# Row statistics gathered four chunks at a time, and an earlier bf16 copy for half of the second FFN's weights, in a macaron conformer layer on eight cores

## The chip, the cores and the metric

One Trainium2 chip, all 8 cores. Each core computes one of the 8 batch rows; the cores exchange nothing. The metric is the device time of the slowest core, in microseconds (us). Engines are named as in the profile: PE (TensorE), DVE (VectorE), ACT (ScalarE), POOL (GpSimd) and SP (SyncE); the last two mostly issue transfers (DMAs).

## What is computed

x is 8 x 4096 x 1024 in float32, the layer has one level, and every product sums over the channels:

```
h = h + 0.5 * swiglu(rmsnorm(h), w_gate, w_up, w_down)        # FFN 1, width 2816
u = rmsnorm(h);  z = u @ w_in                                 # 1024 -> 7 * 1024
a = a_val * sigmoid(a_gate)
a = silu(layernorm(causal_depthwise_conv31(a) + b)) @ a_w_out
y = (b_B * causal_depthwise_conv3(b_C * b_x)) @ b_w_out
h = h + (sigmoid(g_a) * a + sigmoid(g_b) * y) @ w_o           # the mixer
h = h + 0.5 * swiglu(rmsnorm(h), ...)                         # FFN 2, width 2816
out = rmsnorm(h)
```

Both FFNs and the mixer have float32 weights of their own, which the kernel uses as bf16.

## The kernel before

**Tiles.** The 4096 positions of a core are 8 tiles of 512. A tile lives transposed: 8 chunks of 128 channels x 512 positions. For every tile there are three pieces of work: FFN 1, the mixer and FFN 2. `units` (in `_run`) lists the FFN units in the order (0,1), (1,1), (2,1), (3,1), (0,2), (4,1), (1,2), (5,1), (2,2), ... where (t,2) is FFN 2 of tile t. `gen_b` walks these units, `gen_a` the first part of the mixer (input projection, convolutions) and `gen_c` its second part. A planner in `_run` chooses at each step which of the three goes on. It carries a clock per engine in a `Tracker`: each operation is recorded with a cost (`cost=`), and a step is taken when its operands are ready by those clocks. The order of every engine's instructions is thus fixed when the program is built, and a changed cost can move the work of all three generators. All operations are issued from one helper, so the profile gives them one line (L416); they are told apart by the names of their tiles.

**Matrix products.** `group` is a chain of 128x128x512 matmuls into one of 8 PSUM banks `ps`. An FFN unit has 22 gate/up steps (16 matmuls each, moving operand `uF`) and 8 down steps (22 matmuls each, moving operand `act`). Products of the mixer read `uM`, `bact` and halves of `acc`.

**Weights.** They come in slabs of 128 x 2048 elements (128 x 1408 for the down projections, `dn1` and `dn2`, two slabs for a step; 128 x 1024 for a third of `win`) into 9 slots `wslot`. A slab is read anew for each tile. At first it is read from the float32 array `wpack` and cast on the way, by a DMA of POOL's queue. At one of its uses the slot is also written back to the array `wbf` in bf16 by a DMA of SP's queue, and from then on it is read from there, by SP's queue and with half the bytes. `write_use` says at which use that happens, counted from 0: for `gu2` and `dn2`, the slabs of FFN 2, it is 1, the second use. FFN 2 of tile 0 thus reads 38 slabs in float32, FFN 2 of tile 1 reads them in float32 again and writes all of them back, and tile 2 is the first to read them in bf16. `slab_at` issues the loads ahead, as slots come free in order, and `_writeback` the copies; a slot that is being written back can't be loaded before that copy has landed. Of the copies, four can be on their way: the fifth makes SP wait for the first.

**Row statistics.** An RMSNorm needs the sum of squares over all 8 chunks. `norm_square` has ACT square one chunk (128 x 512) into one of 7 buffers `sq`, and puts `stat` into the queue `late`. When the planner's clock says that the square is ready, `flush` calls it: `strips` issues four matmuls of PE, which sum the chunk over its channels. They have 32 columns of ones as the weight (`ones`), 128 positions each, and stand in four column groups of the array (`tile_position`), 128*32 in the profile's form. After the eighth chunk `root` makes 1/sqrt, `spread` broadcasts it with 8 matmuls on `sel`, and ACT copies it to `rstdX` or `rstdM`, which DVE multiplies into `uF` or `uM`. `ln_stat` does the same for the mixer's LayerNorm, with a square and a copy of each finished `acc`. The four strips of one chunk between two runs of full matmuls are called a visit here. `norm_square` is called for the next unit's input in `prepare` (14 units), after each down step in `gen_b` (15 units), and for the first and the last unit in other places.

Of the kernel before, what the change touches and what calls it, by code (L numbers as in the profile page):

```python
# [130 lines left out]
NCAST = 4  # L131
NSQ = 7
NACC = 12
# [196 lines left out]
class Norm:  # L330
    def __init__(self, rstd):
        self.rstd = rstd
        self.ps = None
        self.done = False

# [11 lines left out]
class Builder:  # L347
# [206 lines left out]
    def write_use(self, kk):  # L554
        if kk[0] in ("gu1", "dn1"):
            return 0 if kk[1] % 6 == 0 else 1
        if kk[0] in ("gu2", "dn2"):
            return 1
        return 2 if kk[1] % 3 == 1 else 1
# [172 lines left out]
    def new_sq(self):  # L732
        while len(self.late) >= NSQ - 1:
            self.late.popleft()[1]()
        return self.r_sq.next()

    def strips(self, ps, sq, ap, first, last):
        q = ap.shape[1] // 4
        for g in range(4):
            self.tr.op("pe", lambda E: E.matmul(  # L740
                ps.ap[32 * g:32 * g + 32, 0:q], lhsT=self.ones[:, 0:32], rhs=ap[:, g * q:(g + 1) * q],
                start=first, stop=last, tile_position=(0, 32 * g)),
                reads=[self.b_ones, sq], writes=([ps] if first and g == 0 else []), mark=(g == 3), cost=40.0)
        ps.w = ("pe", self.tr.cnt["pe"])
        ps.tw = self.tr.t["pe"] + 200.0
# [30 lines left out]

    def norm_square(self, norm, k, src, on_dve=False):
        tr = self.tr
        if k == 0:
            norm.ps = self.bank(hold=True)  # L780
        sq = self.new_sq()
# [6 lines left out]
        def total(hl):  # L788
            self.spread(norm.ps, hl, QT)
            tr.op("act", lambda E: E.activation(out=norm.rstd.ap, in_=norm.ps.ap, func=AF.Copy),  # L790
                  reads=[norm.ps], writes=[norm.rstd], cost=600)
            self.release(norm.ps)
            norm.finish()

        def stat():
            self.strips(norm.ps, sq, sq.ap, k == 0, k == KC - 1)
            if k == KC - 1:
                hl = self.root(norm.ps, QT)
                self.late.append((tr.ready([hl]), lambda: total(hl)))
        self.late.append((tr.ready([sq]), stat))  # L800

# [143 lines left out]
    def gen_b(self):  # L945
# [3 lines left out]
        for k in range(KC):  # L949
            self.norm_square(n, k, self.b_h[0][k], on_dve=(k % 2 == 1))  # L950
            self.flush()
# [52 lines left out]
    def last_down(self, q, t, h):  # L1004
# [13 lines left out]
        for es, d in steps:  # L1018
# [27 lines left out]
            self.late.append((tr.ready([sq]), stat))  # L1046
            if es == (1,):
# [67 lines left out]
    def mixer(self, t):  # L1115
# [6 lines left out]
        self.conv_left[t] = KC  # L1122
        self.ln_left[t] = 2 * KC
        for j in range(KC):
# [50 lines left out]
    def merge_out(self, t):  # L1175
# [45 lines left out]
        if t == NT - 1:  # L1221
            q = 2 * NT - 1
            h = self.b_h[q % NH]
            for i in range(KC):
# [7 lines left out]
                    reads=[ps, h[i]], writes=[h[i]], cost=690)  # L1232
                self.norm_square(self.norm_1[q], i, h[i])
            self.m_out.add(t)
# [49 lines left out]
    def ln_stat(self, t, j, acc):  # L1284
        tr = self.tr
        if j == 0:
            self.ln_ps[t] = (self.bank(hold=True), self.bank(hold=True))
        S = self.ln_ps[t]

        def stat(ps, b):  # L1290
            self.strips(ps, b, b.ap, j == 0, j == KC - 1)
            self.ln_left[t] -= 1
        sq = self.new_sq()
        tr.op("act", lambda E: E.activation(out=sq.ap, in_=acc.ap, func=AF.Square), reads=[acc], writes=[sq], cost=620)
        self.late.append((tr.ready([sq]), lambda: stat(S[1], sq)))
        cp = self.new_sq()
        tr.op("act", lambda E: E.activation(out=cp.ap, in_=acc.ap, func=AF.Copy), reads=[acc], writes=[cp], cost=620)
        self.late.append((tr.ready([cp]), lambda: stat(S[0], cp)))

    def layer_norm(self, t, acc, aact):  # L1300
# [21 lines left out]
        def second():  # L1322
# [3 lines left out]
            for ps, x in ((S1, lnr), (S0, nmr)):  # L1326
                hl = self.split(x, QT)
                self.late.append((tr.ready([hl]), lambda ps=ps, hl=hl: out(ps, hl)))

# [49 lines left out]
```

How the kernel before makes its waits and increments, by code:

```python
    def _waits(self, eng, reads, writes):  # L214
        toks = {}
        for b in reads:
            if b.w is not None:
                toks[b.w[0]] = max(toks.get(b.w[0], 0), b.w[1])
        for b in writes:
            if b.w is not None:
                toks[b.w[0]] = max(toks.get(b.w[0], 0), b.w[1])
            for t in b.r:
                toks[t[0]] = max(toks.get(t[0], 0), t[1])
        E = self.eng[eng]
        wd = self.waited[eng]
        for sk in sorted(toks):
            val = toks[sk]
            if sk == "pe" and eng == "pe":
                continue
            if wd.get(sk, 0) < val:
                E.wait_ge(self.sem[sk], val)
                wd[sk] = val
# [16 lines left out]
    def op(self, eng, fn, reads=(), writes=(), cost=700.0, mark=True, bg=False, actset=None):  # L249
        if eng == "dve" and not bg and self.fill is not None:
            self.fill(self.ready(reads, writes))
        reads, writes = _flat(reads), _flat(writes)
        self._waits(eng, reads, writes)
        ins = fn(self.eng[eng])
        if mark:
            self.cnt[eng] += 1
            ins.then_inc(self.sem[eng], 1)
            tok = (eng, self.cnt[eng])
        else:
            tok = (eng, self.cnt[eng] + 1)
# [44 lines left out]
    def wait_tok(self, eng, tok):  # L305
        if self.waited[eng].get(tok[0], 0) < tok[1]:
            self.eng[eng].wait_ge(self.sem[tok[0]], tok[1])
            self.waited[eng][tok[0]] = tok[1]
# [14 lines left out]
                def then_inc(_s, sem, val=1):  # L323
                    entry[3].append((sem, val))
```

## Time and profile before

| | us |
|---|---|
| median of 3 runs | 3174.65 (3174.19 to 3315.42) |
| the profiled execution | 3173.24 |
| its span, from the first to the last instruction, slowest core (4) | 3171.7 |
| spans of the 8 cores | 3153.5 to 3171.7 |
| PE busy, of the span | 3076.1 (97%) |
| DVE busy | 2370.8 (75%) |
| ACT busy | 891.5 (28%) |

All rows below are of core 4. A matmul is drawn from its start to a modelled end, 0.38 us for 512 columns, though the next one can start after 0.216 us; so PE can be called busy for a part of a time in which it starts nothing. "DMA" is the mean busy share of the core's 16 DMA engines, and the share of a queue is that of its packets on the same engines. Sizes of the transfers are those of the bf16 or float32 data at the destination.

### The profile page before, as it was taken

To read this page: it belongs to the slowest core of one execution; us is meant where nothing else is said; L and a number is where in the kernel's file an instruction comes from. 1 tells how busy PE (TensorE), PEld (TensorE's weight loads), DVE (VectorE), ACT (ScalarE), POOL (GpSimd) and SP (SyncE) were. 2 spreads that over 40 slices of the span, in tenths; PEclk is the share of its full clock that TensorE was granted. 3 is DMA by queue.
4 is the path that set the end of the run, shared out by engine and by line. 5 is a ranking of instruction groups with operands and counts; after the bars stand their busy time and mean duration, and the time that the engine had idled before them with its cause. 6 is when DMAs were issued, how large, how long until landed. Compare 5 with 4: busy or idle time off the path is not lost.

```text
span 3171.7 us, 48577 instructions; the slowest of 8 cores (3153.5 to 3171.7 us)
## 1 busy us (share of the span) xinstructions
PE 3076.1 (97%) x15640; PEld 1374.2 (43%) x15640; DVE 2370.8 (75%) x3511; ACT 891.5 (28%) x1648; POOL 193.2 (6%) x367
## 2 busy tenths in 40 slices
PE   8989999999989999889999999999999999999998
PEld 3434344444434444334444444444444444444444
DVE  2258898969877889668897989888988599874222
ACT  2222233224312333113323242233232422332221
POOL 1111001001110000000001000000000000000000
PEclk8999999999999999999999999999999999999999
DMA  9999959979999679997466465565574755646452
GB/s 181 186 219 206 251 141 192 216 219 208 189 209 233 209 190 251 226 234 246 148 186 227 138 220 170 169 230 156 157 232 148 228 174 162 209 147 204 126 194 92
DMA packets 182551, 612.59 MB, mean 193 GB/s; under 512 B 20768, under 2 KB 22944, under 8 KB 176544
## 3 DMA queue, kind: packets, MB, share of 16 engines
q1 hardware_dynamic: 134688, 431.58, 42.9%
q0 software_dynamic: 46640, 176.15, 28.3%
q8 instruction: 133, 2.18, 0.3%
q10 hardware_dynamic: 976, 1.74, 0.2%
q14 instruction: 114, 0.93, 0.1%
HBM read 620.89 MB, written 103.81 MB: 228 GB/s over the span
## 4 chain that ended last, share of the span: by engine, by line
PE 82%; DMA 14%; DVE 2%; issue 1%; ACT 0%; SPq 0%; DVEq 0%; POOL 0%; ACTq 0%; POOLq 0%
PE ps L416 82%; DMA wslot<-wpack 6%; DMA wbf<-wslot 3%; DMA hst<-hs 3%; DMA hs<-hst 1%; DVE acc L416 1%; DMA hT<-xT 0%; DMA wslot<-wbf 0%; SPq L416 0%; DVE hT L416 0%; ACT sq L416 0%; DVE uF L416 0%; DVE fp L416 0%; ACT L416 0%; DVE uM L416 0%
## 5 line engine op out<-in xcount | busy, mean ns | idle before, releaser
L416 DVE SCALAR_TENSOR_TENSOR acc<-abuf,vecs_sb,acc 128x512 f32<-128x512 f32 x1920 | 1435.2, 748 | 132.9 <-ACT acc L416 8.8
L416 PE MATMUL ps<-uF,wslot 128*128 128x512 bf16 x5632 | 1256.4, 381 | 22.1 <-DMA wslot<-wpack 12.9
L416 PEld LDWEIGHTS ps<-uF,wslot 128*128 128x128 bf16 x5632 | 541.8, 98 | 673.3 <-issue 42.3
L416 PE MATMUL ps<-uM,wslot 128*128 128x512 bf16 x3584 | 800.3, 380 | 8.0 <-DVE acc L416 4.6
L416 PE MATMUL ps<-act,wslot 128*128 128x512 bf16 (+1 forms) x2904 | 635.1, 376 | 15.1 <-DMA wslot<-wpack 15.1
L416 ACT ACTIVATE fp<-ps 128x512 f32<-128x512 f32 (+1 forms) x513 | 293.8, 575 | 1024.6 <-PE ps L416 997.0
L416 PEld LDWEIGHTS ps<-uM,wslot 128*128 128x128 bf16 x3584 | 346.1, 98 | 423.1 <-issue 14.7
L416 DVE TENSOR_TENSOR act<-fp,ps 128x512 bf16<-128x512 f32 x352 | 239.9, 684 | 266.1 <-PE ps L416 248.0
L416 PEld LDWEIGHTS ps<-act,wslot 128*128 128x128 bf16 x2904 | 278.2, 98 | 332.7 <-issue 25.8
L416 ACT ACTIVATE sq<-hT 128x512 bf16<-128x512 f32 (+1 forms) x256 | 157.2, 619 | 601.0 <-DVE hT L416 585.4
L416 PE MATMUL ps<-acc,wslot 128*128 128x512 bf16 x1024 | 241.2, 381 | 4.0 <-DVE acc L416 2.3
L416 POOL DMA_DIRECT2D wslot<-wpack x247 | 130.5, 530 | 1255.6 <-PE ps L416 803.6
L416 DVE SCALAR_TENSOR_TENSOR hT<-ps,hT 128x512 f32<-128x512 f32 (+1 forms) x140 | 94.2, 673 | 148.3 <-PE ps L416 148.0
L416 PEld LDWEIGHTS ps<-acc,wslot 128*128 128x128 bf16 x1024 | 97.6, 98 | 120.7 <-issue 6.7
L416 ACT ACTIVATE thg<-ps 128x512 f32<-128x512 f32 x128 | 75.1, 595 | 218.7 <-PE ps L416 191.3
L416 DVE SCALAR_TENSOR_TENSOR fp<-thg,ps 128x512 f32<-128x512 f32 x128 | 87.3, 684 | 52.3 <-PE ps L416 51.3
L416 PE MATMUL ps<-bact,wslot 128*128 128x512 bf16 x512 | 120.9, 379 | 0.0
L416 ACT ACT_TABLE_LOAD x79 | 101.4, 1283 | 65.7 <-PE ps L416 44.8
L416 PE MATMUL ps<-sq,ones 128*32 128x128 bf16 (+1 forms) x1568 | 78.0, 228 | 30.0 <-ACT sq L416 30.0
L416 ACT ACTIVATE sq<-acc 128x512 bf16<-128x512 f32 x128 | 73.5, 621 | 119.0 <-DVE acc L416 118.9
L416 PEld LDWEIGHTS ps<-sq,ones 128*32 128x32 bf16 x1568 | 34.1, 94 | 157.3 <-issue 157.1
L416 DVE SCALAR_TENSOR_TENSOR fp<-cx,vecs_sb,fp 128x512 f32<-128x512 f32 x128 | 95.3, 745 | 0.0
(57 smaller groups left out, 963.9 us busy)
## 6 DMA issues: line engine op xcount, KB each, us to landing
wslot<-wbf SPq DMA_DIRECT2D x470, 512.0 KB, 4.5
wslot<-wpack POOLq DMA_DIRECT2D x170, 512.0 KB, 15.4
wslot<-wbf SPq DMA_DIRECT2D x195, 352.0 KB, 3.3
wbf<-wslot SPq DMA_DIRECT2D x80, 512.0 KB, 11.0
wslot<-wpack POOLq DMA_DIRECT2D x61, 352.0 KB, 15.8
outT<-hT POOLq DMA_DIRECT2D x14, 1024.0 KB, 7.6
hst<-hs POOLq DMA_DIRECT2D x56, 256.0 KB, 5.4
hst<-hs SPq DMA_DIRECT2D x48, 256.0 KB, 7.6
```

What stands on the lines that cost most here:

```text
L416: ins = getattr(E, meth)(*a, **kw)
```

## The change

Four things are changed.

- **Four chunks per visit.** `norm_square` keeps the chunks and calls the new `quad` after each fourth one. `quad` takes 4 `sq` buffers, has ACT do the 4 squares one after the other, and queues one `stat` that issues 16 strips in a row. `ln_stat` does so for its copies and its squares. The ring `sq` grows from 7 to 9 buffers; `new_sqs` counts the buffers that queued visits hold. The first unit's norm, the one in the last `wo` steps (`plain=True`) and the end (`last_down`) stay as they were.
- **Costs that the planner assumes.** A strip 14 ns (40 before) and 190 ns per visit (none before), a matmul of `spread` 72 ns (90 before). They put work in another order, on all engines.
- **A `fill` call** ahead of `root`, which lets queued DVE work go first while the statistics are on their way.
- **Write-back of FFN 2.** `write_use` is `kk[1] % 2`: slabs with an even number (11 of the 22 `gu2`, 8 of the 16 `dn2`) are written back at their first use, in FFN 2 of tile 0, and read in bf16 from tile 1 on. The others stay as they were.

```diff
-NSQ = 7
+NSQ = 9
+NQ = 4
@@ write_use
         if kk[0] in ("gu2", "dn2"):
-            return 1
+            return kk[1] % 2
@@ Builder
+    def new_sqs(self, n):
+        while sum(x[2] for x in self.late) + n > NSQ:
+            self.late.popleft()[1]()
+        return [self.r_sq.next() for _ in range(n)]
+
+    def quad(self, ps, srcs, func, first, last, then):
+        tr = self.tr
+        sq = self.new_sqs(NQ)
+        for b, src in zip(sq, srcs):
+            tr.op("act", lambda E: E.activation(out=b.ap, in_=src.ap, func=func), reads=[src], writes=[b], cost=620)
+
+        def stat():
+            tr.t["pe"] += 190.0
+            for n, b in enumerate(sq):
+                self.strips(ps, b, b.ap, first and n == 0, last and n == NQ - 1)
+            then()
+        self.late.append((max(tr.ready([b]) for b in sq), stat, NQ))
@@ strips
-                reads=[self.b_ones, sq], writes=([ps] if first and g == 0 else []), mark=(g == 3), cost=40.0)
+                reads=[self.b_ones, sq], writes=([ps] if first and g == 0 else []), mark=(g == 3), cost=14.0)
@@ spread
-                    reads=[self.b_sel, hl], writes=([ps] if n == 0 else []), mark=(n == 7), cost=90.0)
+                    reads=[self.b_sel, hl], writes=([ps] if n == 0 else []), mark=(n == 7), cost=72.0)
@@ norm_square
+        def then():
+            if k == KC - 1:
+                self.fill(tr.ready([norm.ps]) + 400.0)
+                hl = self.root(norm.ps, QT)
+                self.late.append((tr.ready([hl]), lambda: total(hl), 1))
+        if not plain:
+            norm.src.append(src)
+            if k % NQ == NQ - 1:
+                self.quad(norm.ps, norm.src[-NQ:], AF.Square, k < NQ, k == KC - 1, then)
+            return
@@ ln_stat
+        if j % NQ == NQ - 1:
+            for ps, func in zip(self.ln_ps[t], (AF.Copy, AF.Square)):
+                self.quad(ps, self.ln_src[-NQ:], func, j < NQ, j == KC - 1, done)
```

Three places of the instructions' order. First PE, in the down steps of FFN 2 of tile 2 (matmuls on `act`), with the norm of the result; `sq,ones` are strips. Before:

```order
523 L416 MATMUL ps<-act,wslot 128x512 x44
524 L416 MATMUL ps<-sq,ones 32x128 x4
525 L416 MATMUL ps<-act,wslot 128x512 x22
526 L416 MATMUL ps<-sq,ones 32x128 x4
527 L416 MATMUL ps<-act,wslot 128x512 x22
528 L416 MATMUL ps<-sq,ones 32x128 x4
529 L416 MATMUL ps<-act,wslot 128x512 x22
530 L416 MATMUL ps<-sq,ones 32x128 x12
```

The same place now:

```order
331 L418 MATMUL ps<-uF,wslot 128x512 x112
332 L418 MATMUL ps<-uM,wslot 128x512 x40
333 L418 MATMUL ps<-uF,wslot 128x512 x32
334 L418 MATMUL ps<-uM,wslot 128x512 x40
335 L418 MATMUL ps<-act,wslot 128x512 x110
336 L418 MATMUL ps<-sq,ones 32x128 x16
337 L418 MATMUL ps<-act,wslot 128x512 x66
```

The strips of four chunks stand in one visit after the fifth down step, where there was a visit for almost every step. Over the whole program the runs of strips go from 300 to 108, with 1568 strips in both.

Second PE again, where the mixer of tile 2 (`uM`) hands over to FFN 2 of tile 0 (the run on `uF`); `sq,sel` is `spread`, and the one right ahead of `uF` is of a norm. Before:

```order
206 L416 MATMUL ps<-uM,wslot 128x512 x16
207 L416 MATMUL ps<-sq,sel 128x128 x8
208 L416 MATMUL ps<-uM,wslot 128x512 x24
209 L416 MATMUL ps<-sq,ones 32x128 x4
210 L416 MATMUL ps<-uM,wslot 128x512 x40
211 L416 MATMUL ps<-sq,sel 128x128 x8
212 L416 MATMUL ps<-uF,wslot 128x512 x96
```

The same place now:

```order
122 L418 MATMUL ps<-uM,wslot 128x512 x40
123 L418 MATMUL ps<-sq,sel 128x128 x8
124 L418 MATMUL ps<-uM,wslot 128x512 x24
125 L418 MATMUL ps<-sq,ones 32x128 x16
126 L418 MATMUL ps<-uM,wslot 128x512 x40
127 L418 MATMUL ps<-sq,sel 128x128 x8
128 L418 MATMUL ps<-uF,wslot 128x512 x96
```

The two norms that end here are those of FFN 1 of tile 3 (for `rstdM`) and of FFN 2's input (for `rstdX`, which `uF` needs). Before, the `spread` for `rstdX` was the first one, with 64 matmuls on `uM` between it and the run on `uF`; now it is the second one, with none between.

Third SP's queue from the load of x for the unit after next (`hT<-xT`), early in FFN 2 of tile 0, up to the loads of h's chunks (`hst<-hs`); `wbf<-wslot` is a write-back. Before:

```order
99 L416 DMA hT<-xT 128x4096
100 L416 DMA wbf<-wslot 128x2048
101 L416 DMA wslot<-wbf 128x2048
102 L416 DMA wslot<-wbf 128x1024
103 L416 DMA wbf<-wslot 128x2048 x5
104 L416 DMA wslot<-wbf 128x2048
105 L416 DMA wbf<-wslot 128x2048
106 L416 DMA wslot<-wbf 128x1024
107 L416 DMA wbf<-wslot 128x2048 x7
108 L416 DMA hst<-hs 128x512 x4
```

The same place now:

```order
107 L418 DMA hT<-xT 128x4096
108 L418 DMA wbf<-wslot 128x2048 x8
109 L418 DMA wslot<-wbf 128x2048
110 L418 DMA wbf<-wslot 128x2048
111 L418 DMA wslot<-wbf 128x1024
112 L418 DMA wbf<-wslot 128x2048 x4
113 L418 DMA wslot<-wbf 128x2048
114 L418 DMA wbf<-wslot 128x2048 x2
115 L418 DMA wslot<-wbf 128x1024
116 L418 DMA wbf<-wslot 128x2048 x8
117 L418 DMA wslot<-wbf 128x2048
118 L418 DMA wbf<-wslot 128x2048
```

Between the load of x and the first `hst` load there are 24 write-backs where there were 14. The whole program has 120 write-backs in both; loads from `wpack` go from 247 to 228 and those from `wbf` from 713 to 732.

## Rows read from the trace of the kernel before

**Rows 1.** Windows: length, busy us of PE, PEld, DVE, ACT, POOL (instructions), PE clock, DMA share, GB/s.

```profile
0.00:363.20 363.20, 322.88 (x1580) 138.15 (x1581) 192.62 (x290) 87.44 (x163) 47.83 (x94) 0.96 1.00 200
363.20:751.30 388.10, 387.73 (x1997) 173.73 (x1995) 330.26 (x485) 116.99 (x217) 27.98 (x53) 1.00 0.82 203
751.30:994.70 243.40, 225.82 (x1132) 99.91 (x1129) 198.57 (x295) 67.09 (x122) 30.08 (x57) 0.97 1.00 202
...
1163.00:1425.60 262.60, 241.87 (x1193) 105.67 (x1191) 199.53 (x297) 69.58 (x130) 19.53 (x37) 0.97 0.95 239
1425.60:3171.70 1746.10, 1731.10 (x8896) 782.45 (x8892) 1309.94 (x1944) 501.01 (x921) 61.43 (x114) 1.00 0.56 180
```

**Rows 2.** Waits of PE over the span: us in total, times, longest.

```profile
PE ps L416 <- ACT sq L416: 30.0, 10, 11.6
PE ps L416 <- DMA wslot<-wpack: 29.7, 21, 5.6
```

**Rows 3.** Timeline of PE, 1840 to 1960 us: start, length, operation.

```profile
1843.66 17.44 PE L416 MATMUL ps<-uF,wslot 128*128 128x512 bf16 x80
1860.94 1.06 PE L416 MATMUL ps<-sq,sel 128*128 128x128 bf16 x16
...
1901.76 1.89 PE L416 MATMUL ps<-bact,wslot 128*128 128x512 bf16 x8
1903.58 0.35 PE L416 MATMUL ps<-sq,ones 128*32 128x128 bf16 x12
1903.86 3.63 PE L416 MATMUL ps<-uM,wslot 128*128 128x512 bf16 x16
```

**Rows 4.** Timeline of PE, 2430 to 2470 us.

```profile
2442.86 4.92 PE L416 MATMUL ps<-act,wslot 128*128 128x512 bf16 x22
2447.71 0.29 PE L416 MATMUL ps<-sq,ones 128*32 128x128 bf16 x8
2447.94 4.92 PE L416 MATMUL ps<-act,wslot 128*128 128x512 bf16 x22
2452.79 0.24 PE L416 MATMUL ps<-sq,ones 128*32 128x128 bf16 x4
2452.96 4.92 PE L416 MATMUL ps<-act,wslot 128*128 128x512 bf16 x22
```

**Rows 5.** DMA queues and issues (last number: us to landing), 751.3 to 994.7 us.

```profile
q0 software_dynamic: 8517, 28.38, 72.7%
q1 hardware_dynamic: 6658, 20.49, 26.7%
...
wbf<-wslot SPq DMA_DIRECT2D x17, 512.0 KB, 11.1
```

**Rows 6.** DMA queues, 1163 to 1425.6 us.

```profile
q1 hardware_dynamic: 14400, 44.54, 52.3%
q0 software_dynamic: 5677, 18.01, 42.0%
```

**Rows 7.** Waits of POOL, 1163 to 1425.6 us.

```profile
POOL wslot L416 <- DMA wbf<-wslot: 142.3, 17, 22.1
```

**Rows 8.** Timeline of all engines, 915 to 945 us.

```profile
929.19 0.75 DVE L416 SCALAR_TENSOR_TENSOR uM<-hst,vecs_sb,rstdM 128x512 bf16<-128x512 f32 x1 [12.05 <-DMA hst<-hs]
...
936.27 0.30 PE L416 MATMUL ps<-sq,ones 128*32 128x128 bf16 x4 [11.58 <-ACT sq L416]
```

**Rows 9.** Timeline of all engines, 736 to 763 us.

```profile
745.44 0.61 PE L416 MATMUL ps<-sq,sel 128*128 128x128 bf16 x8
...
750.85 0.74 DVE L416 SCALAR_TENSOR_TENSOR uF<-hT,vecs_sb,rstdX 128x512 bf16<-128x512 f32 x1
...
758.41 2.07 DVE L416 SCALAR_TENSOR_TENSOR uF<-hT,vecs_sb,rstdX 128x512 bf16<-128x512 f32 x3
...
760.42 2.75 PE L416 MATMUL ps<-uF,wslot 128*128 128x512 bf16 x12
```

**Rows 10.** Groups by form: busy us, mean ns; idle before.

```profile
L416 ACT ACTIVATE sq<-hT 128x512 bf16<-128x512 f32 x248 | 153.8, 625 | 579.2 <-DVE hT L416 563.6 <-DMA hT<-xT 10.2 <-DMA hT<-hs 5.0
```

More of the change, by code:

```diff
@@ L333, in __init__ @@
         self.ps = None
+        self.src = []
         self.done = False
@@ L732, in new_sq @@
     def new_sq(self):
-        while len(self.late) >= NSQ - 1:
+        return self.new_sqs(1)[0]
+    def new_sqs(self, n):
+        while sum(x[2] for x in self.late) + n > NSQ:
             self.late.popleft()[1]()
-        return self.r_sq.next()
+        return [self.r_sq.next() for _ in range(n)]
[10 more added lines that the diff above has]
+        self.late.append((max(tr.ready([b]) for b in sq), stat, NQ))
     def strips(self, ps, sq, ap, first, last):
@@ L775, in root, with norm_square @@
         return self.split(sd, q)
-    def norm_square(self, norm, k, src, on_dve=False):
+    def norm_square(self, norm, k, src, on_dve=False, plain=False):
         tr = self.tr
@@ L780, in norm_square, with total @@
             norm.ps = self.bank(hold=True)
+        def total(hl):
+            self.spread(norm.ps, hl, QT)
+            tr.op("act", lambda E: E.activation(out=norm.rstd.ap, in_=norm.ps.ap, func=AF.Copy),
+                  reads=[norm.ps], writes=[norm.rstd], cost=600)
+            self.release(norm.ps)
+            norm.finish()
+        def then():
[8 more added lines that the diff above has]
+            return
         sq = self.new_sq()
@@ L786, in norm_square @@
             tr.op("act", lambda E: E.activation(out=sq.ap, in_=src.ap, func=AF.Square), reads=[src], writes=[sq], cost=620)
[L788 to L793, printed above, removed]
         def stat():
+            tr.t["pe"] += 190.0
             self.strips(norm.ps, sq, sq.ap, k == 0, k == KC - 1)
[L797 to L800, printed above, removed]
+            then()
+        self.late.append((tr.ready([sq]), stat, 1))
     def scale_op(self, out, src, vcol, k, norm):
@@ L949, in gen_b @@
         for k in range(KC):
-            self.norm_square(n, k, self.b_h[0][k], on_dve=(k % 2 == 1))
+            self.norm_square(n, k, self.b_h[0][k], on_dve=(k % 2 == 1), plain=True)
             self.flush()
@@ L1045, in stat @@
                     self.strips(nps[e], sq, sq.ap[:, e * H:(e + 1) * H], n == 0, n == KC - 1)
-            self.late.append((tr.ready([sq]), stat))
+            self.late.append((tr.ready([sq]), stat, 1))
             if es == (1,):
@@ L1122, in mixer @@
         self.conv_left[t] = KC
-        self.ln_left[t] = 2 * KC
+        self.ln_left[t] = 4
         for j in range(KC):
@@ L1232, in merge_out @@
                     reads=[ps, h[i]], writes=[h[i]], cost=690)
-                self.norm_square(self.norm_1[q], i, h[i])
+                self.norm_square(self.norm_1[q], i, h[i], plain=True)
             self.m_out.add(t)
@@ L1284, in ln_stat, with done @@
     def ln_stat(self, t, j, acc):
-        tr = self.tr
         if j == 0:
             self.ln_ps[t] = (self.bank(hold=True), self.bank(hold=True))
-        S = self.ln_ps[t]
-        def stat(ps, b):
-            self.strips(ps, b, b.ap, j == 0, j == KC - 1)
+            self.ln_src = []
+        self.ln_src.append(acc)
+        def done():
             self.ln_left[t] -= 1
[L1293 to L1298, printed above, removed]
+        if j % NQ == NQ - 1:
+            for ps, func in zip(self.ln_ps[t], (AF.Copy, AF.Square)):
+                self.quad(ps, self.ln_src[-NQ:], func, j < NQ, j == KC - 1, done)
     def layer_norm(self, t, acc, aact):
@@ L1327, in second @@
                 hl = self.split(x, QT)
-                self.late.append((tr.ready([hl]), lambda ps=ps, hl=hl: out(ps, hl)))
+                self.late.append((tr.ready([hl]), lambda ps=ps, hl=hl: out(ps, hl), 1))
         def out(ps, hl):
```

## The prediction

> **What bounds the kernel now.** I read the windows first, since the busy shares of the whole span mix stages with different limits. PE is the engine that sets the end, and its idle time is not spread evenly [rows 1]. From 363 to 751 us it is idle for 388.10 - 387.73 = 0.4 us, and from 1425.6 us on for 15 us in 1746, most of it at the very end. It is idle for 40 us before 363 us, for 17.6 us from 751 to 995 and for 20.7 us from 1163 to 1426. In just these three stretches the DMA engines are 1.00, 1.00 and 0.95 busy, and elsewhere 0.82 and 0.56. So there are two regimes: in three stretches the DMA engines set the pace, and in the rest every nanosecond of PE counts. The waits say the same: PE waited 29.7 us for slabs read from `wpack` and 30.0 us for squares of ACT [rows 2]. The longest of the latter, 11.58 us, is no lack of ACT: DVE sat 12.05 us in front of an `hst` chunk that the loaded DMA engines brought late, and the sum that ACT had to square was queued on DVE behind it [rows 8].
>
> The three stretches are the first tiles' FFN 1, FFN 2 of tile 0, and FFN 2 of tile 1, which reads its 38 slabs in float32 and writes all of them back. An instruction's stall shows smaller than it is, since a matmul is drawn 0.38 us long and the next can start after 0.216. Counting starts instead of ends I get 20.8 us lost in the second stretch and 28.7 in the third; these I use.
>
> **Visits.** What a visit costs is read from starts, in a place where nothing waits. In a long run a matmul takes (1860.94 - 1843.66) / 80 = 0.216 us [rows 3]. Runs of 22 matmuls with the strips behind them take 2447.94 - 2442.86 = 5.08 us with 8 strips and 5.02 with 4 [rows 4]; 22 x 0.216 is 4.75, so the visits cost 0.33 and 0.27. A run of 8 with 12 strips takes 2.10, and the visit 0.37 [rows 3]. That is 0.21 us for coming and going and 0.055 us for each chunk's four strips, which run side by side. The change leaves the strips (1568) and takes visits away: by the order of PE, cut where the windows are cut, they go from 33 to 8 before 363 us, 33 to 12 up to 751, 24 to 6 up to 995, 17 to 7 up to 1163, 20 to 6 up to 1426 and 158 to 54 in the rest. That is 192 visits fewer, 40 us of PE time.
>
> Where it counts: 21 x 0.21 = 4.4 us (363 to 751), 2.1 (995 to 1163), 2.9 (1163 to 1426) and 104 x 0.21 = 21.8 (the rest). In the first stretch (5.2 us) and in FFN 2 of tile 0 (3.8 us) I count nothing, since the DMA engines set the pace there and PE only waits longer.
>
> Here two sections of the Trainium skill's page TensorEngine Tiling (Array Packing) would give different answers. "Key Properties" says that a change of tiling mode drains the engine, which makes the price one of the visit. "Instruction Overhead" says that each matmul has some 60 cycles of overhead however short it is, which makes it one of the strips, and these stay 1568; by it alone the gain would be none. The rows side with the first: 4, 8 and 12 strips cost 0.27, 0.33 and 0.37 us.
>
> **FFN 2 of tile 0 (the new write-backs).** The price of bytes comes from the queues. From 751 to 995 us, POOL's queue (float32 read, cast) took 72.7% of 243.4 us for 28.38 MB in bf16, 6.2 us per MB; SP's took 26.7% for 20.49 MB, 3.2 us per MB [rows 5]. From 1163 to 1426 us it was 6.1 and 3.1 [rows 6]. The change writes 11 slabs of 0.524 MB and 8 of 0.360 MB at their first use, together 8.65 MB or 27 us of all engines' time. There is no room for it: the two queues already fill the stretch. So FFN 2 of tile 0 becomes 27 us longer. Bounds: 0 us, if slots loaded ahead and the looser stretch behind it (share below 0.82) take it all; 40 us, if each write-back also holds its slot (a copy lands 11.1 us after its issue [rows 5], and POOL, which is strictly in order, waited 142.3 us for such copies where all slabs were written back [rows 7]). I take 27, as the stretch's demand and its length agree today.
>
> **FFN 2 of tile 1 (the gain).** Half of the slabs come in bf16 here: 8.65 MB cost 3.1 instead of 6.1 us per MB, 26 us less, and are not written, 27 us less. The DMA engines' work falls from 0.943 x 262.6 = 248 to 195 us [rows 6], against 262.6 - 28.7 - 2.9 = 231 us of PE work, a share of 0.84. The stretch that looks most like it, 363 to 751 us, has 0.82 and lost 0.4 us [rows 1]. I keep 3 us, because by the order of the issues the middle third still asks for slightly more than PE takes. The waits fall by 28.7 - 3 = 25.7 us, between 13 (half stays, as the DMAs still come in bursts) and 28.7.
>
> **Bursts and late norms.** Four squares behind one another take ACT 4 x 0.625 = 2.5 us [rows 10], so a norm is complete some 1.9 us later than with one. ACT is 28% busy, and the planner puts other groups of matmuls ahead of the visit, so in most places other work covers it; in the piece of PE's order shown, 110 matmuls on `act` stand ahead of the visit. One place has lost its cover: FFN 2 of tile 0. Today the `spread` for `rstdX` starts at 745.44, DVE multiplies `uF` from 750.85 to 760.4 between other work, and PE comes to `uF` at 760.42, just in time, after 64 matmuls on `uM` [rows 9]. Now nothing stands between that `spread` and `uF`. The delay of today, 5.4 us to the first `uF`, then falls on PE, and its first group follows DVE's pace (0.67 us a chunk, eight chunks, against 0.216), 3.6 us more: 9 us, up to 12 with the DVE work queued ahead. The DMA engines load slots meanwhile, in a stretch that they bound, so most of it is no extra time; I take 4 us of it and of all such waits, between 0 and 12.
>
> **The sum.** -4.4 + 27 - 2.1 - 2.9 - 25.7 - 21.8 + 4 = -25.9 us. The profiled execution took 3173.2 us (span 3171.7), so 3147.3; the median is 1.4 us above that execution, which gives 3148 to 3149. I say 3148 us, 0.8% below before. What the write-backs cost in tile 0 and bring back in tile 1 cancel, and what stays is the visits of the stretches in which PE is the bound.
>
> **Rivals.**
> - The early write-backs are free. For: the stretch from 995 us has slack, and the slots are loaded ahead. Against: PE already loses 20.8 us in FFN 2 of tile 0, so there is no lead to spend. It would give 3148 - 27 = 3121 us.
> - The written slots are held (slower than before). Place: FFN 2 of tile 0. A slot with a copy under way can't be loaded, POOL can't pass it, and SP, allowed four copies at a time, can't pass a fifth with its `hst` loads behind, which DVE and then PE wait for as in rows 8. Price: the 27 us of bytes, and x us for each of the 19 new copies. It decides from the point where x is over 1.4 us, for then the stretch costs the 26 us that the sum gains elsewhere on top of its 27. With x = 2 it gives 3148 + 38 = 3186. For: 24 write-backs where there were 14 ahead of the first `hst` load in SP's order, and the 142.3 us of POOL [rows 7]. Against: FFN 2 of tile 1 lives with 42 copies today and is only some 14 us longer than its DMA work (262.6 against 248).
> - The norms come too late. Each of 29 norms in groups of four loses its 1.9 us to PE: +55 us, 3203. Against: the planner has 2 other generators to choose from, and ACT's clock in its model is the measured one (620 and 625 ns).
> - The price of a visit is that of its strips: no gain from visits, 3148 + 31 = 3179. Against: rows 3 and 4.
>
> That the change doesn't do what it says is excluded for its form (108 runs of strips instead of 300 in PE's order, 19 loads fewer from `wpack`).
>
> **How the numbers follow.** My forecast 0.62, free write-backs 0.15, held slots 0.13, late norms 0.06, strips as the price 0.04. The range takes the bounds: low 3120 (free write-backs), high 3178 (held slots in part: 13 us more in tile 0, 13 us of waits left in tile 1, 5 us of late norms, 3148 + 31). Beyond it is about 2 in 10. About 2% is what a measurement of this kernel can tell from no change: faster by that is below 3111, slower above 3238. The forecast and all rivals lie within, so 0.93 for the same; 0.04 for faster (free write-backs together with no waits at all in tile 1 and before 363 us), 0.03 for slower (held slots and late norms together).
>
> **What would show it right or wrong.** In the profile after: PE's strips in visits of 16, about 0.43 us from matmul to matmul less 0.216; FFN 2 of tile 0 some 27 us longer, with a DMA share of 1.00; FFN 2 of tile 1 about 28 us shorter at a share near 0.84 and with hardly a wait for `wpack`; the part behind it 22 us shorter, at the same idle time. Wrong would be: a stretch of tile 0 that keeps its length (first rival), POOL's waits for `wbf` in it far above today's or `hst` waits of many 10 us (second), or PE waiting for `sq` all over the second half (third).

## The result and the profile after

The changed kernel takes 0.9926 of the time of the kernel before, with an interval of 0.9897 to 0.9954: 3148 to 3154 us where the kernel before took 3174 to 3175 beside it. The forecast was 3148. The interval excludes 1, so a change of 0.7% can be told from none here, though the forecast put that mark at about 2%. In some runs the cores of one die ran at a lower granted clock and took some per cent longer; ratios leave these out, and where too few others are left, no ratio is given below.

The profiled execution took 3148.29 us, its span is 3146.7 us on core 5. The windows after, cut at the same places of the work as in [rows 1], with the stretch from 1013 us too (columns as there):

```profile
0.00:350.70 350.70, 303.68 (x1528) 132.66 (x1529) 183.90 (x278) 84.34 (x155) 46.26 (x91) 0.98 1.01 202
350.70:744.20 393.50, 392.00 (x2034) 178.57 (x2032) 331.69 (x487) 117.35 (x221) 27.98 (x53) 1.00 0.84 206
744.20:1013.40 269.20, 229.07 (x1125) 99.48 (x1120) 209.51 (x312) 67.72 (x125) 31.67 (x60) 0.94 0.99 209
1013.40:1192.60 179.20, 168.74 (x881) 75.04 (x874) 141.10 (x205) 49.94 (x99) 4.25 (x8) 0.97 0.71 205
1192.60:1423.20 230.60, 230.60 (x1180) 105.19 (x1177) 191.69 (x287) 65.39 (x124) 11.62 (x22) 1.00 0.87 238
1423.20:3146.70 1723.50, 1708.86 (x8913) 786.20 (x8911) 1311.12 (x1947) 499.38 (x923) 61.47 (x114) 1.00 0.56 181
```

FFN 2 of tile 0 (third row) has grown from 243.4 to 269.2 us, with PE idle for 40 us instead of 17.6 and the DMA share where it was. FFN 2 of tile 1 (fifth row) has shrunk from 262.6 to 230.6 us and has no idle time of PE left, at a DMA share of 0.87. The last row is 22.6 us shorter, though PE is idle in it as long as before (14.6 and 15.0 us): that is work that went, not waiting. (Counted from start to start, PE loses some 6 us more there than before; see the table below.)

The waits of PE over the span, where [rows 2] had two large ones:

```profile
PE ps L418 <- DMA wslot<-wpack: 44.9, 40, 4.8
PE ps L418 <- DVE act L418: 14.4, 3, 12.5
PE ps L418 <- DVE uF L418: 10.7, 4, 9.8
PE ps L418 <- ACT sq L418: 8.5, 4, 6.9
...
PE ps L418 <- DMA wslot<-wbf: 7.9, 2, 7.1
```

The waits for slabs read from `wpack` have grown from 29.7 to 44.9 us, and those for squares of ACT have shrunk from 30.0 to 8.5. Two single waits are new, one of 12.5 and one of 9.8 us. The first is the old wait of [rows 8] in another place: the late `hst` chunk holds DVE, for 22.2 us now where it was 12.1, and now it is `act` rather than a square that is queued behind it. The timeline of all engines, 928 to 955 us:

```profile
935.77 2.32 PE L418 MATMUL ps<-act,wslot 128*128 128x512 bf16 x10 [1.09 <-DMA wslot<-wpack]
946.63 0.75 DVE L418 SCALAR_TENSOR_TENSOR uM<-hst,vecs_sb,rstdM 128x512 bf16<-128x512 f32 x1 [22.18 <-DMA hst<-hs]
...
950.64 4.61 PE L418 MATMUL ps<-act,wslot 128*128 128x512 bf16 x12 [12.55 <-DVE act L418]
```

The second is the late norm. PE's timeline, 744 to 766 us, answers to [rows 9]:

```profile
744.19 8.81 PE L418 MATMUL ps<-uM,wslot 128*128 128x512 bf16 x40
752.83 0.61 PE L418 MATMUL ps<-sq,sel 128*128 128x128 bf16 x8
763.26 3.23 PE L418 MATMUL ps<-uF,wslot 128*128 128x512 bf16 x5 [9.82 <-DVE uF L418]
```

The windows of this place (columns as in [rows 1]) show two things more. The DMA engines stay busy through the wait, 0.98 of the time. And the clock granted to PE falls from 2.4 to 1.2 GHz (1.00 to 0.50) in the wait, while PE does nothing, and stays there until 770 us, some 7 us after PE has started again: the third of these windows holds 11 matmuls and the fourth 24.

```profile
755.00:760.00 5.00, 0.00 (x0) 0.00 (x0) 4.69 (x8) 2.62 (x7) 0.00 (x0) 0.65 0.98 197
760.00:765.00 5.00, 1.58 (x3) 0.31 (x3) 5.00 (x8) 0.00 (x0) 0.00 (x0) 0.50 0.98 188
765.00:770.00 5.00, 4.61 (x11) 1.17 (x11) 4.79 (x8) 0.60 (x1) 0.00 (x0) 0.50 1.00 167
770.00:775.00 5.00, 5.00 (x24) 2.28 (x23) 4.09 (x7) 0.60 (x1) 0.53 (x1) 0.99 1.04 205
```

From start to start, PE loses 10.0 us to this wait, 3.5 us in the eight matmuls of the first group, which come at DVE's pace, and about 1 us in the next eight at the lower clock: 14.5 us in all (mean of the cores with all matmuls).

A visit in the same down projection as in [rows 4] and behind it (PE's timeline, 2430 to 2475 us):

```profile
2429.75 10.96 PE L418 MATMUL ps<-act,wslot 128*128 128x512 bf16 x50
2440.54 3.62 PE L418 MATMUL ps<-uF,wslot 128*128 128x512 bf16 x16
2444.09 0.41 PE L418 MATMUL ps<-sq,ones 128*32 128x128 bf16 x16
2444.43 8.81 PE L418 MATMUL ps<-uM,wslot 128*128 128x512 bf16 x40
```

From 2440.54 to 2444.43 are 3.89 us for 16 matmuls (3.46) and 16 strips: 0.43 us, where four visits of one chunk would take 4 x 0.27.

The whole span by stretch, and in brackets PE's lost time counted from matmul start to matmul start. Each number is the mean over the six cores whose traces hold all matmuls. The cuts are those of the windows; where a planner puts some 40 matmuls (9 us) on the other side of a cut, two neighbours must be taken together. The other columns are kernels of the next section.

| stretch | before | after | quad_only | quad_e4 | all_first | after_eall |
|---|---|---|---|---|---|---|
| to the third unit | 358.8 (51.4) | 347.3 (54.9) | 350.4 (58.0) | 346.6 (54.2) | 351.2 (58.8) | 360.6 (59.2) |
| to FFN 2 of tile 0 | 389.8 (3.5) | 393.6 (3.9) | 394.4 (4.7) | 383.2 (2.1) | 394.1 (4.4) | 384.3 (2.6) |
| FFN 2 of tile 0 | 243.6 (21.3) | 270.1 (52.3) | 257.1 (39.3) | 241.8 (19.1) | 291.9 (74.0) | 250.8 (34.7) |
| FFN 1 of tile 4 | 168.4 (2.3) | 173.1 (9.5) | 165.4 (1.8) | 161.0 (2.9) | 177.9 (14.6) | 164.7 (8.3) |
| FFN 2 of tile 1 | 261.7 (28.2) | 231.2 (1.4) | 261.2 (31.3) | 270.4 (31.2) | 230.6 (0.9) | 244.2 (4.1) |
| the rest | 1739.9 (17.4) | 1719.5 (23.2) | 1719.5 (23.0) | 1722.7 (26.2) | 1719.4 (23.1) | 1719.2 (24.6) |

### The profile page after: what moved, and what is told of

The parts are those of the page before. It is cut to its first block, busy times and chain, and to the rows that moved or that the text cites. A ratio compares the mean times of both kernels' runs of the same rounds, so it can differ in the third digit from the quotient of the medians.

```text
span 3146.7 us, 48667 instructions; the slowest of 8 cores (3134.2 to 3146.7 us)
## 1 busy us (share of the span) xinstructions
PE 3033.0 (96%) x15640; PEld 1377.1 (44%) x15640; DVE 2369.0 (75%) x3511; ACT 884.1 (28%) x1646; POOL 183.2 (6%) x348
## 4 chain that ended last, share of the span: by engine, by line
PE 80%; DMA 16%; DVE 1%; issue 1%; ACT 0%; SPq 0%; POOL 0%; DVEq 0%; POOLq 0%; ACTq 0%
PE ps L418 80%; DMA wslot<-wpack 8%; DMA wbf<-wslot 6%; DMA hst<-hs 1%; DMA wslot<-wbf 1%; DVE acc L418 0%; SPq L418 0%; DMA hs<-hst 0%; DMA hT<-xT 0%; DVE uF L418 0%; DVE hT L418 0%; ACT sq L418 0%; ACT L418 0%; DVE fp L418 0%; DVE uM L418 0%
## 5 line engine op out<-in xcount | busy, mean ns | idle before, releaser
L418 PE MATMUL ps<-act,wslot 128*128 128x512 bf16 (+1 forms) x2904 | 626.7, 375 | 33.3 <-DMA wslot<-wpack 16.3
L418 ACT ACTIVATE sq<-hT 128x512 bf16<-128x512 f32 (+1 forms) x256 | 147.6, 617 | 419.7 <-DVE hT L418 413.3
L418 POOL DMA_DIRECT2D wslot<-wpack x228 | 120.5, 530 | 1241.2 <-PE ps L418 866.1
L418 DVE SCALAR_TENSOR_TENSOR uF<-hT,vecs_sb,rstdX 128x512 bf16<-128x512 f32 x128 | 87.2, 747 | 1.8 <-ACT rstdX L418 1.8
L418 PEld LDWEIGHTS ps<-bact,wslot 128*128 128x128 bf16 x512 | 50.1, 98 | 60.4
```

Of the source, the lines that this page charges most:

```text
L418: ins = getattr(E, meth)(*a, **kw)
```

## The experiments

The chips differ: the kernel before took 3171 to 3179 us in most runs, but some 3187 us on the chip of the first four experiments. Ratios are free of this, since each is to the kernel before on the same chip. Stretches of two columns are not: which of them hold the 12 us isn't known. The columns `before`, `after`, `quad_e4` and `after_eall` are of chips on which the kernel before takes 3174 to 3175 us, `quad_only` and `all_first` of the slower one. In FFN 2 of tile 0 and the FFN 1 behind it this matters little: `late_wb` and `late_half`, which like `quad_only` copy no slab of the second FFN there, take 256.4 and 255.5 us and 165.3 and 164.6 us on a faster chip, `quad_only` 257.1 and 165.4.

**The parts of the change.** `quad_only` is the changed kernel with `write_use` as before:

```diff
         if kk[0] in ("gu2", "dn2"):
-            return kk[1] % 2
+            return 1
```

> The grouped visits and the planner's costs, with the second FFN's write-backs where they were. My theory (the visits are the whole net gain, the write-backs cancel): 3148 us, within 4 of the changed kernel; FFN 2 of tile 0 lasts 244 us and FFN 2 of tile 1 about 259 (262 less 2.9 for visits). Rival (the gain comes from the earlier write-backs, the visits only fill waits): 3165 us or more.

Ratio 0.9935 (0.9915 to 0.9954): 21 us. Where my expectation took the grouped visits to be the whole gain of 0.7 to 0.8%, they are most of it, together with the planner's costs, which `quad_only` keeps; the rival's 3165 us was the time on a chip on which the kernel before took 3187, so its number can't be used against mine. But one stretch missed by far: FFN 2 of tile 0 took 257 us, not 244, with the write-backs where they had been. 18 us more are lost there than before, and no copy is to blame.

`wb_only` is the kernel before with `return kk[1] % 2` and nothing else.

> The kernel before with the earlier write-backs alone. My theory: 3174 us within 5, FFN 2 of tile 0 27 us longer, FFN 2 of tile 1 26 us shorter. Rival: 3155 us or less, if the early copies are what gained, or above 3190 if copies need the shorter visits beside them.

Ratio 0.9975 (0.9963 to 0.9987), 8 us less than before, so the copies alone are no loss, and do better than my "within 5". Their order has 13 visits fewer (287 runs of strips, not 300), some 2.7 us of the 8. FFN 2 of tile 0 with the FFN 1 that follows lost 17 us more, and all that comes behind lost some 14 us less (31.5 against 45.6), so by stretches the two cancel. The two ratios added give 0.991, the changed kernel's is 0.9926, inside their intervals.

**Is the price of a visit that of coming and going?** `pairs` groups two chunks instead of four.

```diff
-NQ = 4
+NQ = 2
@@ mixer
-        self.ln_left[t] = 4
+        self.ln_left[t] = 2 * KC // NQ
```

> The changed kernel with two chunks per visit instead of four: 167 runs of strips instead of 108, the same 1568 strips. My theory (0.21 us for each coming and going): 59 x 0.21 = 12.4 us of PE, of which about three quarters fall where PE is the bound, so 9 us above the changed kernel, 3158 us. Rival (the price is per strip, or what gains is the planner's new costs): no more than 2 us above it.

Ratio 0.9970 (0.9957 to 0.9983), 14 us above the changed kernel by the ratios (0.9970 - 0.9926, of 3180 us), against 9 expected and at most 2 by the rival. The 59 visits more have a price though the strips are the same 1568. That it is more than 9 comes in part from waits for squares, 16 us in the mean over the cores where the changed kernel has 2.6 (all waits over 0.1 us that end with a strip, from 60 to 3100 us). The kernel before has 24 us of these: the change takes them away too, beside the visits. The two intervals are too wide to tell 14 us from 9.

**The dose of early copies.** `all_first` has `return 0` for all 38 slabs.

> The changed kernel with all 38 slabs of the second FFN written back at their first use. My theory (27 us per 8.65 MB where the DMA engines are full, and nothing left to gain in FFN 2 of tile 1, which lost only 1 to 3 us): FFN 2 of tile 0 lasts 297 us instead of 270, 3176 us in all. Rival 1 (held slots): the second half of the copies costs more than the first, over 3190 us. Rival 2 (symmetry of cost and gain goes on): 3150 us.

Ratio 0.9968 (0.9937 to 0.9998). FFN 2 of tile 0 and the FFN 1 behind it take 21.8 + 4.8 = 26.6 us more than after, and nothing is gained elsewhere, which is the theory's 27. The time doesn't say so: 0.9968 is 13 us above the changed kernel (0.9926) and not 27, and the theory's 3176 us would be a ratio of 1.000, just outside the interval. The first rival (over 3190) falls by both. The second (3150) falls by the stretch, which is 21.8 us longer. That the second half of the copies costs the bytes in full, as the stretches have it, is likely but not shown; by the ratios it is half of that, with room for either.

**What are the 18 us in `quad_only`?** In that stretch PE waited 9.8 us for `uF`, the wait of the timeline above, with 14.5 us lost in and behind it. On each of six cores it lasted 9.80 to 9.82 us, in the changed kernel, `quad_only`, `all_first`, `late_wb` and `late_half`, and it is in neither the kernel before nor `wb_only`. A wait that doesn't depend on the bytes comes from the order: the planner squares one chunk of the next unit's input per step, and here it is a whole group of steps late. `quad_e4` is `quad_only` with four squares per step for this one norm, and no other edit:

```diff
-            self.norm_square(n, self.sq_k, h[self.sq_k])
+            for _ in range(4 if q == 4 else 1):
+                self.norm_square(n, self.sq_k, h[self.sq_k])
+                self.sq_k += 1
             self.sq_wait = tr.t["pe"] + 1500.0
-            self.sq_k += 1
```

> quad_only, and for the input of FFN 2 of tile 0 alone the squares are called four at a time in one of the planner's steps instead of one per step, so that the norm is complete some 80 matmuls earlier in PE's order. My theory (10 us of PE's wait for uF there are lost for good, though the DMA engines are full): the wait of 9.8 us is gone, the 1120 or so matmuls from the mixer's last projection on take 245 us instead of 257, and the kernel is 10 to 12 us faster than quad_only. Rival (the stretch is set by the DMA engines, so the wait only moves): the same time as quad_only, within 3 us, with more waits for wpack.

Ratio 0.9912 (0.9891 to 0.9934) against 0.9935: 7 us, with intervals that touch. The stretch settles it. It takes 241.8 us for 1128 matmuls and strips, `quad_only` 257.1 for 1120, and it lost 19.1 us instead of 39.3, less than the kernel before. PE's timeline of `quad_e4` there shows the two `spread` with full matmuls ahead of and between them and no wait:

```profile
727.16 5.35 PE L418 MATMUL ps<-uM,wslot 128*128 128x512 bf16 x24
732.35 3.62 PE L418 MATMUL ps<-uF,wslot 128*128 128x512 bf16 x16
735.81 0.61 PE L418 MATMUL ps<-sq,sel 128*128 128x128 bf16 x8
736.25 13.98 PE L418 MATMUL ps<-uF,wslot 128*128 128x512 bf16 x64
```

The ratio rests on three times, 3139, 3150 and 3150 us. In the two longer ones some cores had a lower granted clock (see the last section), and 3139 alone is 0.9888 of the kernel before, 15 us below `quad_only`.

The rival said that in a stretch that the DMA engines fill, such a wait is made up. Here it wasn't, and the kernel before could have told. Its DMA engines are busy all through the stretch, but in the 174 us from 751 to 925 PE had one wait for a slab:

```profile
PE ps L416 <- DMA wslot<-wpack: 1.7, 1, 1.7
```

The loads kept up, so there were no waits for loads that a longer wait in front could have taken the place of. Nor could POOL use the time to get ahead, as its timeline in the changed kernel shows, 725 to 785 us:

```profile
750.57 2.86 POOL L418 DMA_DIRECT2D wslot<-wpack  x5 [1.64 <-DMA wbf<-wslot]
753.60 0.53 POOL L418 DMA_DIRECT2D wslot<-wpack  x1 [0.17 <-PE ps L418]
771.62 0.53 POOL L418 DMA_DIRECT2D wslot<-wpack  x1 [17.49 <-PE ps L418]
```

Six loads were issued at once at the start of PE's wait, and the next one 17.5 us later, when PE had freed a slot. The DMA engines had enough to do with these (0.98 busy in the wait); the lead that PE could gain is bounded by the slots.

**Both together.** `after_eall` is the changed kernel with four squares per step for every unit's input (`range(4)` without the condition).

> The changed kernel with the squares called four at a time for every unit's input. By my theory the wait for uF goes (10 us) and the write-backs cost and gain as before: 10 us below the changed kernel. Rival: equal to it, since the stretch has more bytes to move here than in quad_e4 and the DMA engines set its length.

Ratio 0.9892 (0.9875 to 0.9910), the lowest ratio of all, with an interval that excludes the changed kernel's value: 11 us below it, theory 10. FFN 2 of tile 0 lost 34.7 us instead of 52.3.

But the 11 us don't come from where the theory had them. PE's lost time, counted along the order of its 15640 instructions (the wait for `uF` stands near the 3600th, the one behind the late `hst` chunk between the 4400th and the 4800th; mean of six cores, us):

| PE's instructions | before | wb_only | quad_only | quad_e4 | after | after_eall |
|---|---|---|---|---|---|---|
| 3400 to 4400 | 1.8 | 19.1 | 17.3 | 6.1 | 25.4 | 25.7 |
| 4400 to 5500 | 22.1 | 22.1 | 25.7 | 16.4 | 38.5 | 18.0 |

Without early copies (`quad_only` against `quad_e4`), 11 us of the wait for `uF` come back with the early norm, and 9 us more behind it. With them (`after` against `after_eall`) nothing comes back: the wait is gone, and PE loses as much to slabs that are late. `wb_only`, with the copies and without that wait, loses 19.1 us there, and only 6 us less than the changed kernel. The order of `after_eall` differs in other places too, so this is one comparison and not a proof. PE's waits of `after_eall`, 740 to 1020 us:

```profile
PE ps L418 <- DMA wslot<-wpack: 17.9, 12, 6.7
PE ps L418 <- DVE acc L418: 5.4, 3, 4.6
```

So in the changed kernel the rival was right about this wait, as far as these runs tell. What `after_eall` gains lies behind it, at the `hst` chunk: DVE's longest wait for one is 20 to 25 us in the changed kernel, 8 to 11 in `after_eall` (10 to 14 before, 16 to 19 in `quad_only`), and of PE's wait of 12 to 16 us for `act` no more than 2.5 us is left. That the sum met the theory's 10 us is luck. Why the chunk comes earlier there wasn't tried.

**The planner's costs.** `old_costs` has 40 ns a strip, nothing per visit and 90 ns for a matmul of `spread`, and the rest of the change.

```diff
@@ quad, norm_square
-            tr.t["pe"] += 190.0
@@ strips (line shortened)
-mark=(g == 3), cost=14.0)
+mark=(g == 3), cost=40.0)
@@ spread (line shortened)
-mark=(n == 7), cost=72.0)
+mark=(n == 7), cost=90.0)
```

> The changed kernel with the planner's old costs (40 ns a strip, nothing per visit, 90 ns for a matmul of the broadcast). The visits are the same 108 runs. My theory: the costs only shift the order, within 4 us of the changed kernel, 3150. Rival: they carry part of the gain, 3158 us or more.

It gave one usable time, 3162 us, and no usable profile. So it was run again as `old_costs2`.

> The kernel of old_costs again: the changed kernel with the planner's old costs. The visits are the same 108 runs. My theory: the costs only shift the order, within 4 us of the changed kernel (ratio 0.9926 to before). Rival: they carry part of the gain, a ratio of 0.996 or more.

Ratio 0.9965 (0.9949 to 0.9981), 12 us above the changed kernel where my theory allowed 4: it falls, though the two intervals touch at 0.995. By the stretches it is 11 us more lost time. The costs carry half of the change's 24 us, with the same 108 runs of strips. Most of that lies behind FFN 2 of tile 1, which takes 1732 us instead of 1719.5 and loses 36 instead of 23. A part that can be named is waits for squares: 10 us in the mean over six cores (as counted for `pairs`) against 2.6. For a visit of 16 strips the old costs say 16 x 0.040 = 0.64 us, the new ones 16 x 0.014 + 0.19 = 0.41, and the trace has 0.43. So with the old costs the planner's clock of PE is ahead of the real one, and groups are called when their squares are not finished, as in PE's waits over that kernel's span:

```profile
PE ps L418 <- ACT sq L418: 14.7, 13, 5.6
...
PE ps L418 <- DVE act L418: 7.2, 6, 3.8
PE ps L418 <- DVE uF L418: 6.5, 4, 5.7
...
PE ps L418 <- ACT cx L418: 5.2, 1, 5.2
```

The others are single waits for DVE and ACT. Which cost made which difference wasn't tried.

**Copies at later uses.** If a copy costs only where the DMA engines are full, it should be free in the later tiles. `late_wb` has `return 1 + kk[1] % 3`, `late_half` has `return 1 + kk[1] % 2`, and `late_both` is `late_wb` with `return 2 if kk[1] % 3 == 0 else 1` for the first FFN.

> The changed kernel with the second FFN's slabs written back at their second, third or fourth use, a third each, instead of the first or second. If the cost of a copy is only that of the bytes in a stretch where the DMA engines are full, then moving copies to the later tiles, where they are 0.56 busy, is free: FFN 2 of tile 0 back to 244 us (26 less), FFN 2 of tile 1 keeps a share of about 0.9 and loses 5 us instead of 1.4, FFN 2 of tile 2 does not grow (share below 0.9). 3126 us. Rival (a cast read costs PE time wherever it stands, or POOL's queue is late behind copies): 3140 us or more.

> The same with half at the second and half at the third use. FFN 2 of tile 1: DMA work 222 us against 231 of PE, it loses about 8 us; FFN 2 of tile 2: 53 us more DMA work, a share near 0.9, loses 2 us. 3130 us by the theory of bytes; 3145 or more if it fails.

> late_wb, and the slabs of the first FFN too: a third at the third use, the others at the second, none at the first (before: a sixth at the first). The DMA work before 363 us falls by about 18 us and the stretch up to 751 us takes about 33 more (share 0.82 to 0.91). By the theory of bytes 15 us below late_wb, 3111 us; if the stretch up to 751 us has no such room, equal to late_wb or above.

`late_wb` has 0.9919 (0.9895 to 0.9943), `late_half` 0.9931 (0.9908 to 0.9954), no better than the change. FFN 2 of tile 0 took 256 us in both, as in `quad_only`, so the copies had gone and the late norm stayed; FFN 2 of tile 1 lost 5.7 and 10.6 us, as expected. But FFN 2 of tile 2 lost 21.5 and 19.4 us, where the theory had 0 and 2. From some 1550 us on, the `hst` loads are in POOL's queue, and there they now stand between the cast reads. The timeline of all engines of `late_wb`, 1684 to 1703 us:

```profile
1684.69 0.75 DVE L418 SCALAR_TENSOR_TENSOR uM<-hst,vecs_sb,rstdM 128x512 bf16<-128x512 f32 x1 [5.99 <-DMA hst<-hs]
...
1690.48 0.75 DVE L418 SCALAR_TENSOR_TENSOR uM<-hst,vecs_sb,rstdM 128x512 bf16<-128x512 f32 x1 [4.43 <-DMA hst<-hs]
...
1696.15 0.53 POOL L418 DMA_DIRECT2D wslot<-wpack  x1 [3.79 <-DMA wbf<-wslot]
...
1698.28 0.75 DVE L418 SCALAR_TENSOR_TENSOR uM<-hst,vecs_sb,rstdM 128x512 bf16<-128x512 f32 x1 [4.94 <-DMA hst<-hs]
```

DVE waits for three chunks in a row. It is not that POOL stands still in front of slots being written back (5.0 us in all from 1640 to 1880 us). The chunks take longer: from 1640 to 1880 us POOL's queue is busy for 37.7% instead of 14.3%, and an `hst` load takes 12.4 us from issue to landing instead of 8.3 (medians of core 0, `late_wb` and the changed kernel). So the theory of bytes was too simple for late copies: it counted room on the DMA engines (0.77 busy there) and forgot the small loads that share a queue with the cast reads. No run moved these loads to another queue, so this cause is argued and not shown. `late_both` took 3146 and 3155 us, where 3111 was expected. Up to the third unit it gained nothing: the first stretch took 356 us for 40 instructions more than the changed kernel's 347.

**Late copies with the early norm.** `both_e4` is `late_both` with the squares of `quad_e4`, `both_eall` with those of `after_eall`; `both_e4b` repeats the first, which had given one usable time (3131 us).

> late_both (write-backs spread over later uses for both FFNs) with the squares of that one norm called four at a time. If the wait for uF and the first tiles' bytes are separate losses, it beats all others: some 10 us below late_both, 3110 to 3135 us on a chip where the kernel before takes 3175 to 3185. If the late write-backs only move the loss into FFN 2 of tile 2, where late_wb lost 21 us, it is no better than quad_e4.

> The kernel of both_e4 again. Separate losses: a ratio of 0.986 to before, 10 us below after_eall (0.9892). If the late copies only move the loss into FFN 2 of tile 2: 0.990 or more.

> late_both with the squares called four at a time for every unit's input, after_eall's way. Against after_eall it differs only in when slabs are written back. If the write-backs before 995 us cost what the term of 27 us says, at least 15 us of that comes back and 8 are lost in FFN 2 of tile 2: ratio 0.986. If that term was half as large, equal to after_eall, 0.989.

`both_e4b` has 0.9922 (0.9880 to 0.9965): five runs of 3133 to 3137 us, 0.987 of the kernel before and close to the 0.986 of separate losses, and four of 3156 to 3172 (see the last section). The ratio mixes the two groups. `both_eall` has one time, 3137 us, and no ratio. Its FFN 2 of tile 0 takes 232.9 us for 1088 instructions and loses 17.7, against 250.8 for 1112 and 34.7 in `after_eall`: 17 us come back when no slab is copied at its first use. 6 of them go in the stretch ahead of it and 5 in FFN 2 of tile 1. Over the whole span it loses 8.5 us less than `after_eall`. Whether it beats `after_eall` in time stays open.

## Why the prediction was right in its total, and where it wasn't

**The total** came out at 3148 to 3154 us against 3148, and its first reason holds: the visits in the stretches that PE bounds. The rest of the sum is right in part by luck. The planner's costs had no term and carry 12 us, the copies of FFN 2 of tile 0 cost less than their term, and late norms and late chunks cost more.

**The planner's costs: the step that failed first.** The prediction put them at nothing, and gave no reason. Undone, they cost 12 us, half of the net gain, with the visits unchanged. What I put down to 192 visits fewer is thus the work of both. The prediction's "in most places other work covers it" (the squares of a group) holds for the changed kernel, with 2.6 us of waits for squares, but not with the old costs, with 10 us, and "the rest" then loses 36 us instead of 23. Why is argued only, from the 0.64 us that the old costs give a visit of 16 strips and the 0.43 that it takes: the planner's clock of PE runs ahead by 0.2 us per visit. Which of the three costs does it wasn't tried.

**Visits: right.** 0.43 us for 16 strips as predicted, "the rest" 20.4 us shorter (21.8), with 6 us more lost there. The two stretches before FFN 2 of tile 0 gained 11.5 - 3.8 = 7.7 us together, where the terms had 0 and 4.4. `pairs` shows that the number of visits matters at an equal number of strips; the price of a visit is read from the starts.

**FFN 2 of tile 1: right.** -25.7 and -2.9 us forecast, -30.5 measured, loss 1.4 us at a share of 0.87; the comparison with a stretch of like share held.

**FFN 2 of tile 0: right sum, wrong terms.** This stretch and the FFN 1 behind it grew by 26.5 + 4.7 = 31.2 us, and the terms had 27 + 4 - 2.1 = 28.9. But `quad_only` has 13.5 - 3.0 = 10.5 of these without any early copy, where the terms had 4 - 2.1. The copies cost the other 13.0 + 7.7 = 20.7, where the term had 27. It was too large because PE isn't bound by the loads all through the stretch, as its single wait of 1.7 us in the first 174 us shows; a DMA share of 1.00 says that the engines are busy, not that PE waits for them.

**The late norm: the second step that failed.** The place was right. The size was not: I had 9 us, 5.4 of waiting and 3.6 at DVE's pace, and PE lost 14.5, 10.0 of waiting, 3.5 at DVE's pace and 1 at the lower clock. Of "in a stretch that they bound, so most of it is no extra time; I take 4 us of it and of all such waits" the first half is wrong where slabs are copied as before (`quad_e4`: 11 us come back with the early norm) and, as far as one comparison tells, right in the changed kernel (`after_eall`: none comes back). The second half, "of all such waits", is what failed there: the wait behind the late `hst` chunk, of which I had the row in the kernel before, grew from 12 to 22 us on DVE, and PE lost 38.5 us from its 4400th to its 5500th instruction instead of 22.1. With the squares called early it loses 18.0.

**The rivals.** Free write-backs: true for 6 of the 27 us, refuted as a whole. Held slots: POOL's waits for copies from 744 to 1013 us (84.2 us) are near those before (80.2), and the whole is not slower; but its other half, `hst` loads that come late so that DVE and then PE wait, did happen, for 10 us more on DVE. `quad_only` has 16 to 19 us of it without any early copy, so the copies aren't its only cause. Late norms: one place of 29 in the changed kernel. Strips as the price: refuted by `pairs`. Of the two sections of the Trainium skill's page TensorEngine Tiling (Array Packing) that the prediction sets against each other, "Key Properties" (a change of tiling mode drains the engine) agrees with this trace: 0.43 us for 16 strips in one visit, 4 x 0.27 in four. By the other section, "Instruction Overhead" of the same page of the Trainium skill (some 60 cycles for each matmul), `pairs` and the changed kernel, with the same strips, would not differ.

## What to carry to other kernels

Before you call a wait hidden because the transfers are busy, look for the waits that it would take the place of. Where PE hardly waits for loads behind it, the wait is lost in full, at a DMA share of 1.00 too; where PE does wait for loads, it can be hidden, and taking it away then gains nothing there. A stretch that meets its forecast can do so by other waits than the ones of the forecast, so follow the lost time along the order of the instructions before you name the cause. A planner with assumed costs is part of the kernel: a change in the form of the work calls for new costs, and these were worth half of the net gain here. And when room for a transfer is looked for in a later stage, look at the small loads that share its queue as well as at the bytes.

## What was not expected of the hardware

- Strips in the same visit start 3 ns apart within a chunk and 0.055 us from chunk to chunk, at 4, 8, 12 and 16 strips alike, so the 0.21 us for entering and leaving is what a group saves in work. The first strip starts 0.31 us after the last full matmul, where the next full matmul would start after 0.216.
- The wait for `uF` was the same to 0.02 us on six cores of each of five kernels: a chain of DVE and ACT work, though the DMA engines were full around it. With the old costs it is 5.7 to 6.1 us, with pairs 0.95.
- Each of the two long waits of the changed kernel brought the granted clock down to 1.2 GHz, on every core for 10 to 17 us, in the first until 7 to 8 us after PE had started again. Over the span, matmuls at that clock cost the changed kernel 13 us and the kernel before 17.
- Some cores were granted 0.81 of the clock for a single stretch: cores 2 and 3 in the profiled execution of `quad_e4` for 161 us from 1346 us on, cores 0 and 1 in that of `after_eall` for 163 us from 32 us on. These were the slowest cores of `quad_e4` (3137 and 3148 us against 3116 to 3133) and of `after_eall` (3144 and 3141 us against 3116 to 3136); the first row of its column in the table holds some of it.
- The kernel before differed by 0.4% from one chip to another (3175 and 3187 us), at the same granted clock (0.99): half of the effect studied here.
- The same program (`both_e4b`) gave times in two groups 0.6% and more apart, with cores of one die at a granted clock of 0.98 in every run of the longer group. That such a stretch at 0.81 stands behind it, as in `quad_e4`, is likely: 161 us at 0.81 lower the mean by 0.01. These runs left no trace.
